# Linear attention cut into pieces between the attention's units, gates as tangents, one group-norm statistic for four heads

## What is computed

```python
def mixer(z, ...):
    h = z @ w_in
    (q_a, k_a, v_a, r_a, lr_f, lr_b, q_b, k_b, v_b, g_a, g_b) = jnp.split(h, SPLIT_POINTS, axis=-1)
    a = gla_branch(q_a, k_a, v_a, r_a, lr_f, lr_b, gla_w2, gla_b2, gla_gn)
    b = attention_branch(q_b, k_b, v_b, q_norm, k_norm, cos, sin)
    y = (jax.nn.sigmoid(g_a + b_merge[0]) * (a @ w_pa)
         + jax.nn.sigmoid(g_b + b_merge[1]) * (b @ w_pb))
    return y @ w_out
```

## Time and profile before

| | |
|---|---|
| median of 3 runs | 2989.55 us (2989.28 to 2990.94) |
| profiled execution | 2986.32 us, span 2984.5 us |
| TensorE busy | 2657.3 us, 89% of the span |
| VectorE, ScalarE, GpSimd busy | 31%, 30%, 30% |
| mean granted clock of TensorE | 0.943 |

### The profile page before, as it was taken

One profiled execution on the slowest core, in us unless ns is written; L12 is line 12 of the kernel. 1 busy time (PEld: TensorE's weight loads), 2 busy tenths in 40 slices (PEclk: granted clock), 3 DMA queues, 4 the chain that ended last, 5 costly groups with the idle time before them and its releaser, 6 DMA issues.

```text
span 2984.5 us, 44784 instructions
## 1 busy us (share of the span) xinstructions
PE 2657.3 (89%) x18090; PEld 2033.1 (68%) x18090; DVE 914.5 (31%) x2235; ACT 902.4 (30%) x1470; POOL 887.9 (30%) x373
## 2 busy tenths in 40 slices
PE   7999997899999999879989689999878687999996
PEld 7987566799999766779989644444447584444443
DVE  2201523521111152252217332332223613323233
ACT  4330461334343136224433121211113521121112
POOL 5860001578678200146867100000014340000000
PEclk9999996999999999789999799999988988999999
DMA  6563220354554332124555489999953145999995
GB/s 220 170 185 113 86 85 29 113 170 154 171 170 160 125 113 73 41 85 146 165 162 167 169 348 421 421 421 422 421 195 104 57 185 236 421 421 421 421 421 220
DMA packets 271019, 643.94 MB, mean 216 GB/s; under 512 B 16672, under 2 KB 190880, under 8 KB 221472
## 3 DMA queue, kind: packets, MB, share of 16 engines
q1 hardware_dynamic: 267808, 635.66, 56.7%
q10 hardware_dynamic: 2176, 3.15, 0.4%
q0 software_dynamic: 896, 3.15, 0.3%
HBM read 637.72 MB, written 4.19 MB: 215 GB/s over the span
## 4 chain that ended last, share of the span: by engine, by line
PE 76%; DMA 11%; DVE 9%; ACT 2%; issue 1%; ACTq 0%; SPq 0%; POOL 0%; DVEq 0%
PE bank L532 35%; PE bank L496 14%; DMA wring<-in_exp_w 10%; PE bank L988 6%; PE bank L973 5%; PE bank L949 3%; PE bank L997 3%; PE bank L962 3%; PE bank L784 2%; PE bank L564 1%; PE bank L701 1%; PE bank L506 1%; DVE ARENA L1710 1%; DVE ARENA L1509 1%; DVE ARENA L1599 1%
## 5 line engine op out<-in xcount | busy, mean ns | idle before, releaser
L1760 POOL TENSOR_TENSOR wring_rounded<-wring,wring_rounded 128x1024 fp32r<-128x1024 f32 (+1 forms) x336 | 859.5, 2561 | 484.9 <-ACT wring_rounded L1062 484.5
L532 PE MATMUL bank<-SQ_rounded,wring_rounded 128*128 128x272 f32 (+1 forms) x3456 | 659.6, 291 | 35.1 <-DVE XN_rounded L1346 30.9
L532 PEld LDWEIGHTS bank<-SQ_rounded,wring_rounded 128*128 128x128 f32 x3456 | 550.8, 191 | 39.9 <-issue 18.1
L1062 ACT ACTIVATE wring_rounded<-wring 128x1024 fp32r<-128x1024 f32 (+1 forms) x336 | 374.8, 1118 | 504.7 <-PE bank L532 479.2
L532 PE MATMUL bank<-ARENA_rounded,wring_rounded 128*128 128x272 f32 (+1 forms) x3456 | 450.4, 294 | 60.5 <-DVE ARENA_rounded L1501 27.6
L532 PE MATMUL bank<-XN_rounded,wring_rounded 128*128 128x272 f32 (+1 forms) x1728 | 500.5, 290 | 0.0
L532 PEld LDWEIGHTS bank<-ARENA_rounded,wring_rounded 128*128 128x128 f32 x3456 | 447.1, 195 | 64.3 <-DVE ARENA_rounded L1501 28.5
L532 PEld LDWEIGHTS bank<-XN_rounded,wring_rounded 128*128 128x128 f32 x1728 | 331.8, 192 | 0.0
L988 PE MATMUL bank<-wring,ARENA 128*32 128x512 f32 x2048 | 248.0, 602 | 42.1 <-DVE ARENA L1710 30.3
L1284 ACT ACTIVATE ARENA<-bank 128x512 f32<-128x512 f32 x128 | 76.4, 597 | 661.0 <-PE bank L988 661.0
L496 PE MATMUL bank<-XN,wring 128*128 128x272 f32 (+2 forms) x1088 | 257.2, 401 | 11.8 <-DVE XN L1353 11.8
(11 more groups left out here) (232 smaller groups left out, 2310.7 us busy)
## 6 DMA issues: line engine op xcount, KB each, us to landing
wring<-in_exp_w SPq DMA_DIRECT2D x256, 1024.0 KB, 18.5
ARENA<-in_exp_w SPq DMA_DIRECT2D x128, 1024.0 KB, 17.1
wring<-in_ffn_w_gate SPq DMA_DIRECT2D x44, 1024.0 KB, 5.5
wring<-in_ffn_w_up SPq DMA_DIRECT2D x44, 1024.0 KB, 8.1
wring<-in_ffn_w_down SPq DMA_DIRECT2D x32, 1408.0 KB, 6.2
wring<-in_w_in SPq DMA_DIRECT2D x16, 2048.0 KB, 7.8
wring<-in_conv_w_in SPq DMA_DIRECT2D x24, 512.0 KB, 5.3
wring<-in_attn_w_in SPq DMA_DIRECT2D x5, 2048.0 KB, 9.1
```

The costliest lines, as they stand in the source:

```text
L532: ins = nc.tensor.matmul(o, rounded(a_[:, k, cols]), rounded(x), start=(start and k == 0 and j == 0), stop=(stop and k == len(tiles) - 1 a ...
L1062: st.done(A(rounded(high), w_, ACT.Copy), wh_ready)
L1760: st.done(nc.gpsimd.tensor_tensor(rounded(low), low, part(high), ALU.subtract), wl_ready)
```

## The change

It does the following, in both mixers.

- The GLA's products are cut into pieces that stand between the attention's units: keys turned in steps 1 to 3, scores of the two directions in steps 4 and 5, the meta tokens' in 6, states in 7 to 10, one head's output each in 12, 14, 16 and 18, the means in 24. The gate tiles move to other steps so that gates and pieces alternate in banks 6 and 7 (`SPARE_BANK`). TensorE waits for the decayed keys before the loop's first step.
- The two directions' masked scores are added by VectorE, so that a head's output has one product per chunk with the values instead of two. States and head outputs claim both spare banks before they start.
- The means of the four heads go into 32 rows each of one bank; one root and one reciprocal serve all four, and four products with a row of ones spread the result over the 128 rows again. The product with silu(r) comes before the normalisation, the gain with it.
- The gates are `tanh(x/2)`, used as `(1 + tanh) * product`, with the factor 0.5 moved into the sum into H; the bias is halved once.
- `pb` comes before `pa`: first two chunk pairs of `pb`, then the four products that spread the deviation, then the other two, then `pa`. The weights are loaded in that order. The first three high parts are made in steps 22 to 24.

```diff
-        tall(("pa", l), w["w_pa"][l], 4)
         tall(("pb", l), w["w_pb"][l], 4)
+        tall(("pa", l), w["w_pa"][l], 4)
...
-            for kk in range(4):
-                for x in (label, ("pb", label[1])):
+            for x in (("pb", label[1]), label):
+                for kk in range(4):
...
+GATE_STEPS = (0, 1, 3, 5, 6, 8, 10, 11, 13, 15, 17, 19, 20, 21, 22, 23)
+KEY_STEPS = (1, 2, 3)
+SCORE_STEPS = (4, 5)
+META_STEP = 6
+STATE_STEPS = (7, 8, 9, 10)
+OUT_STEPS = (12, 14, 16, 18)
+MEAN_STEP = 24
...  TensorE:
+                def states(i):
...
+                    for b_ in (6, 7):
+                        claim(b_)
...
+                def head_out(h):
...
+                    for b_ in (6, 7):
+                        claim(b_)
+                    for c in range(4):
...
+                        by_row[r0].append((o, VA[r0:r0 + 64, t, h * P:h * P + P], ATT[r0:r0 + 64, 2 * h + t, :]))
...
+                def head_means():
+                    st.need(sq_ready, 4)
+                    products(0, "act", "act", [[(bank[0][32 * h:32 * h + 32, 0:T], const("mean128")[:, 0:32], OSQ[:, h, :])]
+                                               for h in range(4)])
...
                 scores(0)
+                st.need(gla_ready)
                 for n in range(len(units) + 2):
...
+                st.need(xl_ready, 4)
+                for kk in range(2):
+                    gated_products(kk, pairs(BTH, BT, 4))
+                st.need(d2p)
+                for h in range(4):
+                    b = (6, 7, 0, 1)[h]
+                    products(b, "dve", "dve", [[(bank[b][:, 0:T], const("ones")[32 * h:32 * h + 1, :],
+                                                 OSTD[32 * h:32 * h + 1, :])]])
+                for kk in range(2, 4):
+                    gated_products(kk, pairs(BTH, BT, 4))
                 st.need(d2p)
                 for kk in range(4):
+                    gated_products(kk, pairs(ATH, AT, 4))
                 st.need(d2p)
...
+            def gated_products(kk, tiles):
+                for i in range(2):
+                    b = 2 + 2 * (kk % 2) + i
+                    claim(b)
+                    chunk_done(split_sum(bank[b][:, 0:T], tiles, cols=slice(i * P, i * P + P), again=(i == 1)),
+                               bank_full["dve"][b])
+                    held[b] = "dve"
...  ScalarE:
-                st.done(A((GA, GB)[g // 8][:, g % 8, :], bank[b][:, 0:T], ACT.Sigmoid,
+                st.done(A((GA, GB)[g // 8][:, g % 8, :], bank[b][:, 0:T], ACT.Tanh, scale=0.5,
...
+                    if n in (22, 23, 24):
+                        high_part()
+                st.need(bank_full["act"][0])
+                st.done(A(OSTD, bank[0][:, 0:T], ACT.Sqrt, bias=const("eps_rms")), a2d)
...  VectorE:
+                st.need(a2d)
+                st.done(v.reciprocal(OSTD, OSTD), d2p)
...
+                def head_scaled(h):
...
+                    st.done(STT(rounded(ATH[:, h, :]), AT[:, h, :], g, bank[b][:, 0:T], ALU.mult, ALU.mult))
+                    then(STT(AT[:, h, :], AT[:, h, :], g, bank[b][:, 0:T], ALU.mult, ALU.mult), bank_free["dve"][b])
                     st.done(TT(rounded(AT[:, h, :]), AT[:, h, :], part(ATH[:, h, :]), ALU.subtract),
                             None if h < 3 else d2p)
...
+                for kk in range(2):
+                    gated(GB, kk)
+                for h in range(4):
+                    head_scaled(h)
+                for kk in range(2, 4):
+                    gated(GB, kk)
+                for kk in range(4):
+                    gated(GA, kk)
+                    st.settle()
+                    for k in (2 * kk, 2 * kk + 1):
+                        then(TT(GA[:, k, :], GA[:, k, :], GB[:, k, :], ALU.add))
+                        then(v.tensor_copy(rounded(GAH[:, k, :]), GA[:, k, :]))
+                        st.done(TT(rounded(GA[:, k, :]), GA[:, k, :], part(GAH[:, k, :]), ALU.subtract),
+                                None if k < KD - 1 else d2p)
...
-                    st.done(TT(H[:, k, :], bank[b][:, 0:T], H[:, k, :], ALU.add), h_tile)
+                    st.done(STT(H[:, k, :], bank[b][:, 0:T], 0.5, H[:, k, :], ALU.mult, ALU.add), h_tile)
```

268 lines of the change are left out of this document (137 added, 131 removed).

## The result

| | before | after |
|---|---|---|
| median of the runs | 2989.4 us (4 runs) | 3008.3 us (3005.7 to 3010.4, 4 runs) |
| profiled execution, span | 2986.3, 2984.5 us | 3007.9, 3006.1 us |
| TensorE busy; mean granted clock | 2657.3 us; 0.943 | 2678.9 us; 0.935 |
| attention loop, first and second mixer | 112.7, 112.5 us | 163.2, 168.4 us |
| loop's end to the output products, first mixer | 98.3 us | 49.5 us |

The ratio is 1.0063 with a 95% interval of [1.0046, 1.0081]: slower. 2941.5 us had been forecast, within 2920 to 2966.

The account below looks back on a forecast made before the run. TensorE bounds the loop, VectorE's chains and the half clock the rest. Loop 30.4 us longer, then 43.9 to the output products: 24.0 earlier, 48 for two mixers; 2986.3 becomes 2938.2, with 3.2 for the median 2941.5 us, range 2920 to 2966.

Parts of the forecast that it names:

- The full clock in the loop: Head outputs moved into the attention loop run at clock 1.00: 106 ns a record, 11.9 us, bounds 11.8 to 14.3.
- part 2: What the attention loop gains in length: 3.5 + 8.5 + 11.9 + 2.0 + 4.5 = 30.4 us per mixer.
- turns, scores and states at their present prices: These pieces, moved into the attention loop, cost what they cost before at clock 1.00: 8.5 us.
- Rival 1: In the loop only the head outputs lose the full clock: 11.9 us more per mixer, 2965 us; chance 0.08.
- rival 2: Loop steps 12 to 19 stay at half clock through bank waits: 42 us more per mixer, 3025 us; chance 0.03.
- The 24 us from which it decides: Half clock's loss per mixer from which rival 2 was said to decide the result.
- The first wait: Wait for the decayed keys, moved ahead of the loop: 3.5 us more, bounds 2.7 and 6.
- Stalls: New waits in the loop, for bank claims and head outputs' drains: 4.5 us in all, bounds 1 and 9.
- rival 3: Each of eight two-bank claims in the loop costs 1.5 to 2 us: 12 to 14 more per mixer, 2967; chance 0.09.
- Behind the loop: Stretch from the attention loop's end to the output products: 43.9 us, bounded by VectorE.
- Table loads: ScalarE's table loads in the loop go if Exp and Tanh share a table; TensorE doesn't wait for them, nothing counted.
- Behind them nothing changes: Everything behind the start of the output products was taken to stay the same.

Follow-up runs that it names:

- v_mix: v_block with the first pair of `pb` moved ahead of the head outputs; 2960.8 us, ratio 0.9906 to the kernel before.
- x_dense: The changed kernel with each head's 14 output products replaced by 7 of 272 columns (result not right, times only); 2965.6 us, ratio 0.9920 to the kernel before.
- x_claim: The changed kernel with one bank claimed ahead of states and head outputs in place of two; 2997.3 us, ratio 1.0027 to the kernel before.
- x_wait: The changed kernel with TensorE's wait for the decayed keys moved from ahead of the loop to behind step 1; 3000.8 us, ratio 1.0042 to the kernel before.
- b_tanh: The kernel before with only the gates changed, to tangents in place of sigmoids; 2988.9 us, ratio 0.9999 to the kernel before.
- v_block: The changed kernel with the linear attention taken out of the loop into one stretch behind it; 2964.0 us, ratio 0.9923 to the kernel before.

## Why the prediction was wrong

It fell short by 66.8 us (3008.3 for 2941.5). By its own steps:

- **The full clock in the loop: the step that failed.** In part 2 I halved the head outputs' 211 ns because they "began at the half level, after idle time". v_mix has them begin at the full level with 0.28 us of idle time or none, and they are at half 2.6 us later; x_dense, with other products in their place, has 1.00 where the changed kernel has 0.75. The earlier trace rows held the sign: in 30.5 us of them the clock never came back. I read it as an effect of the wait before. The row that I set against it, 12 us of small products at 1.00, was of scores, transposes and states, and I carried it to another kind of product. Nor does that row hold for its own kind: the 64 records of states take 3.82 us in it and 5.96 in v_mix's second mixer. So the term "turns, scores and states at their present prices" failed with it, at a smaller price: gate tiles behind them take 5.4 to 6.5 us in the changed kernel, 2.5 us more in all in the first mixer and 4.7 in the second.
- **Who pays for it.** Rival 1 let only the outputs lose the clock. The low clock lasts through the unit and the gate tile behind each: gate tiles of 5.5 to 6.9 us in place of 3.9. The loops took 163.2 and 168.4 us where 143 was forecast, 20 and 25 us more. This is rival 2's effect at about half its size (42 us per mixer), though not by its reason, waits on banks. The 24 us from which it decides are no more than the forecast gain; the loops' losses lie to both sides of them, and the 5 us lost behind the loops make both mixers slower, by 1.6 and 7.2 us. I gave it 0.03, since it put the low level on all of steps 12 to 19 and I looked for rows that excluded all of it, not for ones that excluded half.
- **The reason I gave rival 2.** The Trainium skill, "TensorE: Matmul & The Clock Gate", section "A second HAM failure mode: psum-queue depth-cycling", would have it from micro-idles between banks. The low clock came, but x_dense has the same banks and waits at 1.00 and x_claim fewer claims at 0.77, so the measurement speaks for the short products instead.
- **The first wait.** 3.5 us forecast, 2.7 to 6 as bounds; idle time grew by 3.2 us and the gate tile behind takes 6.11 us, where the tile behind the wait took 4.94 before. x_wait, which undoes it, is 4.2 us ahead at the first states: the term was right within its bounds. The first loop then gains nothing from it and the second 4.1, so it can't be had back one for one.
- **Stalls.** 4.5 us forecast for the claims; idle ahead of the states is 1.47, 0.58 and 0.67 us, 2.7 in all, and x_claim measured 3.4 to 4.0 us per mixer for the second claim. Right in size; rival 3, 12 to 14 us, is out.
- **Behind the loop.** 43.9 us forecast, 49.5 and 48.8 measured. The start of `pb` (4.0, measured 4.05) and its second half (E + 14.8, measured E + 13.1) are right; the spread of the deviation takes 0.74 us, not 2.0. Missing are a third collision with GpSimd while the heads are scaled, and the half clock on the first pair of `pa`, behind an idle time of 4.32 us for which I had 1. The windows of the first 4.25 us of `pb` and of the first 5.8 us of `pa`, and three rows of VectorE:

```profile
510.25:514.50 4.25, 4.25 (x19) 4.25 (x20) 0.89 (x2) 0.00 (x0) 4.25 (x2) 0.50 0.18 67
...
529.81:535.60 5.79, 5.79 (x26) 5.79 (x27) 1.39 (x5) 0.00 (x0) 0.00 (x0) 0.52 0.49 187
```

```profile
520.23 2.31 DVE L1570 TENSOR_TENSOR ARENA_rounded<-ARENA,ARENA_rounded 128x272 fp32r<-128x272 f32 x1
...
536.88 2.61 DVE L1585 TENSOR_TENSOR ARENA_rounded<-ARENA,ARENA_rounded 128x272 fp32r<-128x272 f32 x1
...
539.88 2.47 DVE L1584 CAST ARENA_rounded<-ARENA 128x272 fp32r<-128x272 f32 x1
```

  Both starts are at half clock; I had counted this for `pb` alone. A rounded subtraction that takes 0.44 us undisturbed takes 2.31 and 2.61 beside GpSimd's low part, a cast of 0.30 us 2.47. Seven of the eight low parts from 516 us on hit one VectorE operation each, for 1.3 to 2.2 us, 1.8 on average; each of the seven ends 0.2 to 0.3 us after GpSimd's. The 1.57 us for each low part, worked out from means, were about right; what was left out is how many fall on the heads.
- **Table loads**: nothing forecast, nothing measured (b_tanh).
- **Not in the prediction at all**: the second stack. "Behind them nothing changes" was true of the code and not of the time: +8.9 us in the second experts' stage from the longer gap at the loop's exit.

By the profiled executions it is 69.7 us (3007.9 for 2938.2): 20.2 + 25.4 for the loops, 5.6 + 4.9 behind them, 8.9 in the second experts' stage and 3.9 in all other stages are 68.9. The 3.9 has no cause found; b_tanh, with TensorE's program and gaps of before, differs from before by 4.3 us in the second experts' stage alone, so a few us in a stage of one execution say little. v_block shows what the rest of the change brings: 16.4 us per mixer, of which 15.9 are read behind its first loop.

## What to carry to other kernels

Work that is moved into a full loop can bring its own clock with it. Before short products are put beside dense ones, look in the trace for a place where the same products follow dense work, and if there is none, move one dense chunk ahead of them and see (one kernel, as v_mix), in both mixers, for one place at full clock doesn't promise the next. What they lower is paid by what stands behind them, so leave them in one place where little stands behind, or between chunks that wait anyway. And when a result is off in a stage that wasn't edited, compare the stages before the story: the exit of a loop with a run-time length can cost more or less with the length of the program ahead of it.

## What the runs showed that was not expected

- TensorE's clock fell to 0.50 with TensorE busy nearly all the time: 18.49 of 18.80 us busy in v_mix at 0.50, 67.0 of 68.0 at 0.75 in the changed kernel; the same places with half as many products, of 272 columns: 65.1 of 66.0 at 1.00.
- The same 64 records of states took 3.82 us in the first mixer of v_mix and 5.96 in the second, behind the same products.
- The idle time at the exit of a loop with run-time length was 2.1 to 2.4 or 5.1 to 5.9 us, and 98 or 90 instructions more ahead of it changed it from 5.5 to 2.1. With the clock behind it that was worth 8 to 11 us each time (3008.3 to 2998.1, 2960.8 to 2952.8, 2954.6 to 2943.9), of which 7 to 9 are read in the stage itself.
- A gain of 4.4 us at one place of a full loop (x_wait, first mixer) was given back within 30 us by the clock; in the second mixer it was kept.
